# Low parts of two memory rows: from GpSimd to VectorE, behind the third convolution tile

## The reference, cut to what matters

```python
n = rms_norm(h, ln_mix_pre[l])
(da_q, ..., dn_q, dn_k, dn_v, ..., ca_q, gate_logits) = [n @ wp for wp in jnp.split(w_in[l], SPLIT_IDX, axis=-1)]
qkv = short_conv(jnp.concatenate([dn_q, dn_k, dn_v], axis=-1), conv_w[l])
mkv = rms_norm(mem, mem_norm_g[l]) @ w_mem_kv[l]
gates = jax.nn.sigmoid(gate_logits.reshape(B, S, N_BRANCH, D_MODEL))
```

## Time and profile before

| | us |
|---|---|
| median of 3 runs | 1347.2 (1346.96 to 1347.26) |
| the profiled execution | 1345.9 |
| its span, first to last instruction | 1344.1 |
| PE busy | 1318.6 (98%) |
| DVE busy | 755.4 (56%) |
| ACT busy | 471.2 (35%) |
| POOL busy | 199.9 (15%) |

### The profile page before, as it was taken

How to read it: one execution, slowest core, us unless ns; L and a number is a source line. 1 busy time by engine, 2 the same in 40 slices (tenths; PEclk the granted TensorE clock), 3 DMA queues, 4 the chain that set the end, 5 groups by cost and what they waited for, 6 DMA issues and landing times.

```text
span 1344.1 us, 24187 instructions
## 1 busy us (share of the span) xinstructions
PE 1318.6 (98%) x10361; PEld 1107.2 (82%) x10361; DVE 755.4 (56%) x1293; ACT 471.2 (35%) x779; POOL 199.9 (15%) x140
## 2 busy tenths in 40 slices
PE   9899999999999999999999999999989999999997
PEld 8689987877888887888878888888988888888786
DVE  6577334576576576577965354554366522355335
ACT  5343433343353444443534222113443312222220
POOL 1123000013000023000321312233112200022000
PEclk9999999999999999999999999999999999999999
DMA  5145412222222232212233636644323333323321
GB/s 216 55 147 184 143 48 95 79 94 65 81 64 79 74 106 89 65 56 102 80 88 96 183 122 222 194 150 148 122 84 120 98 110 95 94 94 97 107 63 63
DMA packets 59601, 143.52 MB, mean 107 GB/s; under 512 B 5048, under 2 KB 24040, under 8 KB 59496
## 3 DMA queue, kind: packets, MB, share of 16 engines
q1 hardware_dynamic: 59496, 141.99, 32.5%
HBM read 127.27 MB, written 16.27 MB: 107 GB/s over the span
## 4 chain that ended last, share of the span: by engine, by line
PE 89%; DVE 6%; ACT 2%; issue 1%; DMA 1%; POOL 0%; SPq 0%; DVEq 0%; ACTq 0%
PE acc L1890 18%; PE acc L1891 17%; PE acc L1892 17%; PE ps_a L1892 2%; PE ps_a L1891 2%; PE ps_a L1890 2%; PE ps_a L1999 2%; PE ps_d L2077 2%; PE ps_d L2210 2%; PE ps_a L2210 2%; PE ps_d L2212 2%; PE ps_a L2212 2%; PE ps_d L2211 2%; PE ps_a L2211 2%; PE acc L2212 1%
## 5 line engine op out<-in xcount | busy, mean ns | idle before, releaser
L1408 DVE TENSOR_TENSOR w_lo<-w_raw,w_hi 128x1024 fp32r<-128x1024 f32 x172 | 235.5, 1370 | 221.4 <-ACT w_hi L1086 220.6
L1086 ACT CAST w_hi<-w_raw 128x1024 fp32r<-128x1024 f32 x172 | 180.1, 1048 | 411.5 <-PE acc L1892 332.1
L1890 PE MATMUL acc<-n_hi,w_hi 128*128 128x512 f32 (+1 forms) x776 | 313.9, 404 | 5.5 <-ACT conv_x L1161 5.0
L1892 PE MATMUL acc<-n_hi,w_lo 128*128 128x512 f32 (+1 forms) x776 | 300.7, 388 | 0.0
L1891 PE MATMUL acc<-n_lo,w_hi 128*128 128x512 f32 (+1 forms) x776 | 300.4, 387 | 0.0
L1890 PEld LDWEIGHTS acc<-n_hi,w_hi 128*128 128x128 f32 x776 | 146.7, 189 | 35.4 <-issue 7.4
L1892 PEld LDWEIGHTS acc<-n_hi,w_lo 128*128 128x128 f32 x776 | 146.5, 189 | 30.5
L1891 PEld LDWEIGHTS acc<-n_lo,w_hi 128*128 128x128 f32 x776 | 147.0, 189 | 26.1 <-issue 0.7
L1074 POOL TENSOR_TENSOR h_lo<-sq,h_hi 128x512 fp32r<-128x512 f32 x32 | 41.4, 1295 | 234.2 <-DVE h_hi L1806 234.2
L1892 PE MATMUL acc<-y_hi,w_lo 128*128 128x512 f32 x192 | 74.7, 389 | 0.0
L1890 PE MATMUL acc<-y_hi,w_hi 128*128 128x512 f32 x192 | 74.7, 389 | 0.0
(11 more groups left out here) (406 smaller groups left out, 2513.9 us busy)
## 6 DMA issues: line engine op xcount, KB each, us to landing
w_raw<-weights SPq DMA_DIRECT2D x200, 512.0 KB, 3.5
gate_scratch<-gate_st SPq DMA_DIRECT2D x24, 256.0 KB, 4.2
g_in<-gate_scratch SPq DMA_DIRECT2D x24, 256.0 KB, 3.9
y_raw<-y_scratch SPq DMA_DIRECT2D x16, 256.0 KB, 3.7
x_tok<-x SPq DMA_DIRECT2D x4, 512.0 KB, 5.1
y_scratch<-y_st SPq DMA_DIRECT2D x4, 512.0 KB, 2.7
y_scratch<-d_ET SPq DMA_DIRECT2D x4, 512.0 KB, 2.9
y_scratch<-y_st SPq DMA_DIRECT2D x8, 256.0 KB, 2.4
```

The costliest lines, as they stand in the source:

```text
L1086: nc.scalar.copy(hi_of_tile(t), w_raw[:, t % RAW]).then_inc(hi_ready, 1)
L1408: V_.tensor_tensor(lo_of_tile(t), w_raw[:, t % RAW], hi_of_tile(t).bitcast(F32), ALU.subtract).then_inc(lo_ready, 1)
L1890: mm(bank, wh, hi_of(k), start=start and k == 0, stop=False)
L1892: last = mm(bank, wl, hi_of(k), start=False, stop=stop and k == KT - 1)
```

## The change

The low parts of rows 4 and 5 leave POOL's list. DVE makes them, in a new step at half tile 9: behind the finish of convolution tile 3 and ahead of the low part of weight tile 7 and the convolution of tile 4. POOL's list then has rows 0 and 2, the gates' scaling, and what follows. The bias matmul and the mk and mv tiles wait for the count of DVE's rows (four of them) in place of POOL's.

```diff
--- before.py
+++ after.py
@@ -178,7 +178,7 @@
 FIRST = 9
 PE_AT = {4: (("ba_rows",),), 5: (("ba",),), 6: (("rows", ST), ("rows", ST + 1)), 14: (("bias",),), 16: (("decay",),)}
 ACT_AT = {4: (("ba",),), 6: (("beta",),), 7: (("rows", ST), ("rows", ST + 1)), 14: (("bias",),), 16: (("decay",),)}
-DVE_AT = {2: (("mem_norm",),), 5: (("beta_in",),), 6: (("mem_gain",),), 12: (("beta",),)}
+DVE_AT = {2: (("mem_norm",),), 5: (("beta_in",),), 6: (("mem_gain",),), 9: (("mem_lo",),), 12: (("beta",),)}
 SP_AT = {15: (("bias", 0),)}
 
 
@@ -734,7 +734,8 @@
         ssd, rsd, tmd = smd[:, 56:64], smd[:, 64:72], smd[:, 72:80]
 
         N_SU = ST + MT
-        POOL_ROWS = (0, 2, 4, 5)
+        POOL_ROWS = (0, 2)
+        LO2_ROWS = (1, 3, 4, 5)
 
         score_parts = {"as0": ((0, 3, 0), (1, 3, 512), (0, 1, 1280)),
                        "as1": ((1, 2, 640), (0, 2, 128), (1, 1, 1280), (0, 0, 0), (1, 0, 512))}
@@ -1457,6 +1458,11 @@
 
                 for j in range(ST, N_SU):
                     gain(j)
+
+            def memory_lo():
+
+                for j in range(ST, N_SU):
+                    row_lo(j)
 
             dve.wait_ge(in_ba, 16)
             V_.tensor_tensor(both, ident[0:4 * HB, 0:2 * HB], ident[0:4 * HB, 2 * HB:4 * HB], ALU.add)
@@ -1681,7 +1687,7 @@
 
             dve_work = {"lo": split_lo, "conv": conv, "fin": finish, "delta": delta, "max": attn, "scale": attn_scale,
                         "pre": reload_hi, "beta_in": beta_and_decay_inputs, "beta": beta_and_decay,
-                        "mem_norm": memory_norm, "mem_gain": memory_gain}
+                        "mem_norm": memory_norm, "mem_gain": memory_gain, "mem_lo": memory_lo}
             for kind, *n in ORDER_OF["DVE"]:
                 dve_work[kind](*n)
 
@@ -1865,7 +1871,7 @@
                 pe.wait_ge(in_oh, 16)
                 pe.wait_ge(in_relb, 16)
                 pe.wait_ge(su_full, N_SU)
-                pe.wait_ge(su_lo, len(POOL_ROWS))
+                pe.wait_ge(su_lo2, len(LO2_ROWS))
                 mm(ps_a[0:HA, 0, 0:SPAN], relb_sb, onehot_sb, start=True, stop=True).then_inc(f_mm, 1)
 
             def keep_awake(n):
```

## The result

The changed kernel takes 1339.5 us (median of 4 runs, 1339.05 to 1340.01) against 1347.2 for the kernel before: ratio 0.9945, 95% interval 0.9931 to 0.996. A second set gave 1340.0 (5 runs) against 1346.6 (15 runs of before): ratio 0.9951, interval 0.9939 to 0.9964. So it is 6.6 to 7.7 us faster; 6.5 was forecast, 1340.7 with a range from 1339.2 to 1343.2. The profiled execution took 1340.0, 5.9 less than that of before.

A forecast was written before the change was run, and what follows sets the result against it. PE's 5.0 us wait ahead of tile 6, from loads held behind POOL's rows, was taken as the bound. Loads 7.94 us earlier less 1.46 for the rows on DVE gave 6.5: 1340.7 us, range 1339.2 to 1343.2.

The forecast's parts named there:

- The slower rival: SP's store is held by something other than POOL, load 6 stays at 54.44, rows are pure cost: 1348.7 us; 4%.
- the price: The two rows on DVE put low part 7 and all DVE work behind it back by 1.46 us.
- 1.14 and 3.10: Time of one row subtraction on DVE: 1.14 us with POOL empty, 3.10 beside a POOL instruction; 1.14 was taken.
- The bound of 6.2: Upper end of the row price on DVE: 6.2 us for the pair, giving 1344.6 us.
- back at 1347.2: Time if the pair took 6.2 and PE's wait ahead of the decay matmuls also brought the low clock's 2.95 us.
- The wait ahead of the decay matmuls: After tile 7, PE waits about 1.1 us for DVE's last decay value, and is 7.0 us ahead.
- the delta product: First product of the delta rule on PE, at 107.42 before; forecast 6.5 us earlier, with everything behind it unchanged.
- the 1340 to 1341.4 that had 70%: Total time in us if the forecast holds as worked out, chance 70%.
- the rival with the rows hidden: Low part 7 is late anyway, so the rows on DVE cost nothing: gain 7.9 us, 1339.3 us; 8%.
- The 2.95 us of low clock: Tile 6 and the bias matmul, behind PE's 5.0 us wait, run at 1.2 GHz: 9.27 us instead of 6.32.
- the 8.1 "to be had": On PE's account: the wait ahead of tile 6, from 59.39 to 64.52, plus 2.95 us of low clock.
- the clock falls in the new wait: Low clock behind PE's wait ahead of the decay matmuls costs another 2.95 us: 4.0 ahead, 1343.2 us; 5%.

The follow-up runs named there:

- the held run: The changed kernel with two extra subtractions left on POOL ahead of the gate scaling, so store and loads stay late: 1348.0 us, ratio 1.0011 to the kernel before.
- the runs with POOL busy: The run with the gate first, and the changed kernel with two extra POOL subtractions timed to run beside DVE's two rows, 1344.7 us.
- the run with the gate first: The kernel before, with POOL scaling the gate of tile 2 first and making rows 4 and 5 behind it, nothing moved to DVE: 1341.4 us.
- the rows moved into the gap: The changed kernel with the two rows two half tiles earlier on DVE, ahead of the low part of weight tile 6: 1338.2 us.
- the run with PE kept busy: The kernel before, with 20 small matmuls on PE during its 5 us wait ahead of tile 6: 1355.3 us, ratio 1.0058.

## Why the prediction was right, point by point

**The loads.** Right to a few hundredths: store 44.96 forecast, 44.98 measured; load 45.34 and 45.36; cast of weight tile 6 at 50.23 and 50.16. The slower rival (loads no earlier) is what the held run sets up, and it gave the price: 1.44, where 1.46 was worked out.

**The rows.** 1.14 each forecast, 56.54 to 58.81 measured, 2.27 for the pair; low part 7 6.55 us earlier than the earlier trace rows. The choice between 1.14 and 3.10 is settled by the runs with POOL busy: 3.33 for a low part beside POOL's rows, 6.76 for two. The bound of 6.2 was too low for the worst case: with two instructions on either side they took turns, 3.42 for each of DVE's. The prediction's "back at 1347.2", for this price and the low clock together, is a slip of the sum (1344.6 and 2.95 make 1347.5); neither bounds the range. The Trainium skill (SBUF — State Buffer, section "Who interferes with whom") says that two such instructions exclude one another; the trace agrees with it: in the run with the gate first the low part on DVE ended 1.08 behind POOL's second row.

**PE.** The wait ahead of the decay matmuls was worked out as 1.1, from where the next matmul could have started; counted so it is 1.09 (71.26 to 72.35), and the profile's 0.93 counts from the end that it gives the last matmul. PE is 7.02 ahead there (7.0 forecast) and 6.54 at the delta product (6.5). That DVE's chain sets the end holds: the rows moved into the gap took 1.5 us off the delta product, rows made twice added 3.2.

**Behind 101 us** the prediction said that nothing changes. In the profiles it does, by PE's short stops: +0.8 at 158, -1.5 from 690 to 701. Which of them the timed runs have can't be seen. Those from 690 to 701 stand among 32x32 matmuls, that at 158 ahead of a matmul of a weight tile; what sets them is open.

**The number.** That 6.5 lies so near to the timed 6.6 and 7.7 is in part luck. Profile against profile the gain is 5.9: the execution was forecast at 1339.4 and took 1340.0, by the stops. The 1.3 from there to the median was that of the kernel before and did not carry over: in the changed kernel the profiled execution lies 0.5 above the first set's median and on the second's. So 1339.5 falls just below the 1340 to 1341.4 that had 70%, and by the time alone it would be the rival with the rows hidden, 1339.3. What decides for the forecast is the mechanism: 2.27 for the pair, low part 7 6.55 earlier, the delta product 6.54.

**What was weighed wrongly.** Two things, neither of which entered the sum. The 2.95 us of low clock stood on PE's account as part of the 8.1 "to be had"; the run with PE kept busy shows, up to the decay matmuls, that without it PE waits there for DVE instead. Its time, longer for other reasons, does not test this. And the rival "the clock falls in the new wait" was put off with "the fall came with a wait of 5". It came with shorter waits too: 1.56, 2.28, 2.56 and 3.17 us ahead of the decay matmuls and 2.72 ahead of tile 7, one profile each, while 0.93 (the changed kernel, two profiles) and 1.41 (the held run) left it at 1.00. So that argument did not carry the 5%; whether the clock fell in any of the changed kernel's timed runs can't be told from their mean clocks, 0.998 and 0.999. Where it fell in tile 8, about 1 us showed at the delta product, not the 2.5 of the rival: the stretch at 0.50 was shorter than before (3.4 us against 6.8), and PE had waits for DVE to lose first. From the decay matmuls to the delta product it takes 28.05 in the kernel before, 28.53 in the changed kernel, where it waits on the way, and 29.43 to 29.50 in the four runs with the fall in between.

## What to carry to other kernels

A queue that issues DMAs in order passes on every wait: here two subtractions of 2.4 us on an idle engine held a small store, and behind it three loads that had nothing to do with it. When a stall of an engine goes, look for the chain that is late next and add the price there: 8.1 us on PE's account became 6.5 because DVE stood right behind. Put the moved work in a stretch in which its new engine stands idle, and see that the two engines' two-input instructions don't run side by side: two half tiles earlier the same rows cost nothing, and the delta product came 1.4 us earlier still.

## What the runs showed of the hardware that I had not expected

The granted clock went to 0.50 behind PE waits of 1.56 to 3.17 us in five runs, over some 3.4 us in each, against 6.8 from 63.8 in the kernel before; and executions of one and the same kernel differ in it (a mean of 0.995 to 0.999 in the run with each row twice). PE stops that nothing in the profile releases came back at the same places in two profiles of one kernel (690, 696 and 701), and in the profile with 20 more matmuls near 60 there are 6.3 us of them later in the run; whether those matmuls brought them was not tried.
